# Differential attention on one core: ScalarE's copies ahead of its exponentials, filling work shifted by a quarter, another accumulator for the last item

## The reference

```python
def one_block(args):
    qi, i = args
    sc = jnp.einsum('bqhcd,bkhcd->bhcqk', qi, k).astype(jnp.float32) * scale
    ...
    p = jax.nn.softmax(jnp.where(mask, sc, NEG_INF), axis=-1)
    a = p[:, :, 0] - lam * p[:, :, 1]
    return jnp.einsum('bhqk,bkhv->bqhv', a.astype(v.dtype), v)
...
og = rms_norm(og, gla_norm_w)
yc = (og.reshape(b, l, D_C) * jax.nn.silu(cg.astype(f32))).astype(h.dtype)
...
y = jnp.concatenate([yc, yd], axis=-1) @ w_out
```

## Time and profile before

| | |
|---|---|
| median of 3 runs | 1270.98 us (1270.24 to 1275.65) |
| the profiled execution's own time | 1270.85 us |
| its span (first to last instruction) | 1269.1 us |
| TensorE busy | 1215.1 us, 96% of the span |
| VectorE busy | 883.4 us, 70% |
| GpSimd busy | 735.7 us, 58% |
| ScalarE busy | 292.1 us, 23% |
| mean granted TensorE clock | 0.988 |

### The profile page before, as it was taken

How to read it: one execution, slowest core, us unless ns; L and a number is a source line. 1 busy time by engine, 2 the same in 40 slices (tenths; PEclk the granted TensorE clock), 3 DMA queues, 4 the chain that set the end, 5 groups by cost and what they waited for, 6 DMA issues and landing times.

```text
span 1269.1 us, 23149 instructions
## 1 busy us (share of the span) xinstructions
PE 1215.1 (96%) x8605; PEld 1150.3 (91%) x8605; DVE 883.4 (70%) x1294; ACT 292.1 (23%) x626; POOL 735.7 (58%) x566
## 2 busy tenths in 40 slices
PE   6969899999999999999999998899999999999995
PEld 6967799999999999999999986799999999999995
DVE  6987588999999941217544688767999999972222
ACT  3015332222222200003111166423222222210002
POOL 6732257676677676666653441256666666666661
PEclk9989899999999999999999999999999999999998
DMA  6310022322322223224222311132322222233221
GB/s 213 117 59 28 26 84 83 100 83 83 96 86 83 90 93 100 91 91 129 84 84 67 102 51 35 34 111 84 98 85 83 93 89 83 86 96 100 88 77 72
DMA packets 35556, 108.92 MB, mean 86 GB/s; under 512 B 5984, under 2 KB 7824, under 8 KB 35504
## 3 DMA queue, kind: packets, MB, share of 16 engines
q1 hardware_dynamic: 29232, 102.51, 25.2%
q10 hardware_dynamic: 6272, 5.67, 1.5%
HBM read 103.04 MB, written 5.13 MB: 85 GB/s over the span
## 4 chain that ended last, share of the span: by engine, by line
PE 88%; DVE 8%; ACT 2%; issue 1%; DMA 0%; POOL 0%; POOLq 0%; ACTq 0%; SPq 0%; DVEq 0%
PE psum L450 18%; PE psum L448 12%; PE psum L449 12%; PE psum L451 11%; PE psum L452 9%; PE psum L437 7%; PE psum L439 7%; PE psum L438 6%; DVE even_winsum L1429 1%; PE psum L789 1%; PE psum L656 1%; DVE small L1650 1%; DVE even_rope_swapped L1411 1%; DVE probs L1500 1%; ACT diff_probs L1142 0%
## 5 line engine op out<-in xcount | busy, mean ns | idle before, releaser
L398 POOL TENSOR_TENSOR w_lo<-w_raw,w_hi 128x1024 fp32r<-128x1024 f32 x187 | 485.9, 2598 | 15.6
L395 POOL TENSOR_TENSOR tick<-tick 1x1 f32<-1x1 f32 x183 | 53.4, 292 | 479.0 <-PE psum L439 240.2
L450 PE MATMUL psum<-h_both,w_hi 128*128 128x480 f32 x704 | 267.1, 379 | 0.0
L448 PE MATMUL psum<-h_both,w_hi 128*128 128x304 f32 x704 | 216.0, 307 | 0.0
L449 PE MATMUL psum<-h_both,w_hi 128*128 128x304 f32 x704 | 212.9, 302 | 0.0
L451 PE MATMUL psum<-h_both,w_lo 128*128 128x304 f32 x704 | 211.0, 300 | 0.0
L396 POOL TENSOR_SCALAR w_hi<-w_raw 128x1024 fp32r<-128x1024 f32 x187 | 197.5, 1056 | 9.5 <-DMA w_raw<-in_weights 8.1
L437 PE MATMUL psum<-h_both,w_hi 128*128 128x272 f32 x608 | 181.2, 298 | 13.6 <-DVE h_both L1241 9.8
L452 PE MATMUL psum<-h_both,w_lo 128*128 128x240 f32 x704 | 191.6, 272 | 0.0
L439 PE MATMUL psum<-h_both,w_lo 128*128 128x272 f32 x608 | 177.1, 291 | 0.0
L438 PE MATMUL psum<-h_both,w_hi 128*128 128x272 f32 x608 | 176.3, 290 | 0.0
(11 more groups left out here) (238 smaller groups left out, 2399.4 us busy)
## 6 DMA issues: line engine op xcount, KB each, us to landing
w_raw<-in_weights SPq DMA_DIRECT2D x187, 512.0 KB, 3.5
x<-in_x SPq DMA_DIRECT2D x8, 272.0 KB, 5.5
out_y<-x SPq DMA_DIRECT2D x8, 272.0 KB, 2.4
out_diff_v_new<-odd_dv ACTq DMA_DIRECT2D x1, 1024.0 KB, 5.3
out_diff_k_new<-odd_kT ACTq DMA_DIRECT2D x1, 1024.0 KB, 4.7
even_rope<-in_rope ACTq DMA_DIRECT2D x1, 544.0 KB, 3.8
odd_rope<-in_rope ACTq DMA_DIRECT2D x1, 544.0 KB, 3.7
consts<-in_consts ACTq DMA_DIRECT2D x1, 384.5 KB, 4.9
```

The costliest lines, as they stand in the source:

```text
L395: pool.tensor_tensor(tick[:, :], tick[:, :], tick[:, :], ALU.mult).then_inc(ticks, 1)
L398: pool.tensor_tensor(w_lo[:, k], w_raw[:, k % RAW], w_hi[:, k].bitcast(F32), ALU.subtract).then_inc(w_ready, 1)
L448: pe.matmul(one, wh, both[:, 0, 0:ONE], start=first, stop=False)
L450: pe.matmul(two, wh, both[:, :, ONE:T], start=first, stop=False)
```

## The change

It has four parts.

- ScalarE: in unit `u` the loop now issues `odd_turned(u)` and then `odd_exp(u + 1)`. Before it issued `odd_exp(u + 1)` in unit `u - 1`, ahead of `odd_turned(u)`.
- TensorE: the filling work of units 9 and later is one step further on. Units 9 to 19 now hold one step at each place. A half chunk ends at place 0 of units 9, 11, 13, 15, 17 and 19, ahead of `odd_scores(u + 2)`, and the next one begins at place 1 of the same unit, behind the scores. Before, it ended at place 1 and the next began at place 0 of the unit after. The step of item 10 (m = 6) that unit 19 takes up is missing behind the loop.
- VectorE: `out_first` now stands between `odd_normalise(u + 1)` (and `head_copy`) and `odd_max(u + 2)`; it stood at the end of the unit.
- The last half chunk (m = 7) goes to accumulator 0 and waits for no `x_upd`; `head_low(4)` stands ahead of its `out_first`.

```diff
         ODD_FILL = {-1: (0, 8), 0: (1, 2), 1: (1, 2), 2: (1, 1), 3: (1, 3), 4: (1, 3), 5: (1, 3), 6: (1, 3),
-                    7: (1, 1), 8: (0, 1), 9: (0, 1)} | {u: (1, 1) for u in range(10, 20)}
+                    7: (1, 1), 8: (0, 1)} | {u: (1, 1) for u in range(9, 20)}
...
-        assert done == 0 and item == 10
+        assert done == 1 and item == 10
...
                     if m == 0:
                         pe.wait_ge(evac, EVEN_IN + ODD_IN)
-                    else:
+                    elif m < KC - 1:
                         pe.wait_ge(x_upd, X_ODD + m)
...
-                    ins = tiles(3, s, [(4 * (m % 2) + c, y_hi[:, c], y_lo[:, c])], c == 0, c == 3)
+                    ins = tiles(3 if m < KC - 1 else 0, s, [(4 * (m % 2) + c, y_hi[:, c], y_lo[:, c])], c == 0, c == 3)
...
             odd_values(19)
-            gla_fill(6, 0, 4)
+            gla_fill(6, 1, 4)
...
             for u, (b, h) in enumerate(OU):
                 odd_turned(u)
+                if 1 <= u < len(OU) - 1:
+                    odd_exp(u + 1)
...
-                if u + 2 < len(OU):
-                    odd_exp(u + 2)
...
                 if h == 0 and b >= 1:
                     head_copy(b - 1)
+                if fill_end.get(u, 0) >= 4:
+                    out_first(S_ODD_OUT, fill_end[u] - 4, KC)
                 if u + 2 < len(OU):
                     odd_max(u + 2)
...
-                if u in fill_end:
-                    if fill_end[u] < 4:
-                        gate_in(fill_end[u])
-                    else:
-                        out_first(S_ODD_OUT, fill_end[u] - 4, KC, 0)
+                if fill_end.get(u, 4) < 4:
+                    gate_in(fill_end[u])
             head_copy(4)
-            out_first(S_ODD_OUT, 6, KC, 0)
+            out_first(S_ODD_OUT, 6, KC)
             head_scale(4)
+            head_low(4)
             out_first(S_ODD_OUT, 7, KC, 0)
-            head_low(4)
```

More of the change, by code:

```diff
@@ L1257, in add_out, with out_first @@
                 ve.tensor_tensor(halves(x[:, m]), halves(x[:, m]), pair(acc), ALU.add).then_inc(x_upd, 1)
-            def out_first(s0, m, mid0, upd0):
-                if m >= 0:
-                    add_out(slab_done if m % 2 else mid_done, (s0 if m % 2 else mid0) + m // 2 + 1, 3, m)
+            def out_first(s0, m, mid0, acc=3):
+                add_out(slab_done if m % 2 else mid_done, (s0 if m % 2 else mid0) + m // 2 + 1, acc, m)
             def out_norm(s0, mid0, n, early):
@@ L1515, in _ @@
                 if u in EVEN_FILL:
-                    out_first(S_EVEN_OUT, EVEN_FILL[u], 0, 0)
+                    out_first(S_EVEN_OUT, EVEN_FILL[u], 0)
                 if c == 0 and b >= 1:
@@ L1521, in _ @@
             for m in range(len(EVEN_FILL), KC):
-                out_first(S_EVEN_OUT, m, 0, 0)
+                out_first(S_EVEN_OUT, m, 0)
             even_low(4)
```

## The result

The changed kernel takes 1276.88 us (median of 22 runs, 1273.47 to 1279.3). In the same sessions the kernel before takes 1273.24 (22 runs, 1270.24 to 1276.6); its first three runs, shown above, had a median of 1270.98. The ratio is 1.0022, 95% interval 1.0013 to 1.0031: slower by about 2.8 us (the two medians are 3.64 apart, inside the interval), which is real and lies within the 0.5% that I called no change.

What follows compares the result with a forecast made beforehand. TensorE, busy 96%, was taken as the bound, with 10.7 us of waits in the stage. 6.6 us lost less 2.45 gained in the tail, added to 1270.85, gave 1275.0; 0.6 for the clock made 1275.6, range 1270.0 to 1280.0.

Steps and rivals of the forecast that it cites:

- ScalarE's order: Copy of unit u ahead of unit u+1's exponentials: 4.21 us a unit instead of 4.74; alone a gain of 1.7 us.
- The fill and `out_first`: At the middle of odd units, `out_first` waits behind normalisation and stalls TensorE: 10.0 us a pair of units against 9.5.
- The collision: In unit 11, GpSimd's split (L398) holds VectorE's L1665 until 793.6, so TensorE stalls 4.2 us.
- the second rival: No collision: L1665 starts ahead of L398 in unit 11; 2.2 us less, no long stall, 1272.3; chance 0.25.
- The clock: Behind the 4.2 us stall TensorE's clock may fall: bounds 0 and 1.6 us, 0.6 taken.
- the stepping: Row lengths followed through all units in the new order; for the old kernel it gave `out_chunk` at 834.0 against 833.86.
- The tail: From unit 19's transposes to `out_chunk`: 10.0 us instead of 12.45, a gain of 2.45.
- The sum: First `out_chunk` 4.15 us later (6.6 - 2.45), giving 1275.0; with 0.6 for the clock, 1275.6.
- The third rival: Stalls of 4.2 and 2.4 us each lower TensorE's clock, 1.6 us each: 1278.2, slower by over 0.5%; chance 0.2.

Runs made afterwards that it cites:

- after_old_act: The changed kernel with ScalarE's old order (exponentials two units ahead, in front of the copy): ratio 1.0016 to the kernel before.
- after_kept_busy: The changed kernel with unit 10's value product repeated six times in unit 11, where TensorE waits for `out_first(1)`: ratio 1.0038 to the kernel before.
- last_only: The kernel before with the last half chunk in accumulator 0, no `x_upd` wait, and `head_low(4)` ahead of its addition: ratio 0.9989.
- before_narrow_split: The kernel before with GpSimd's low part of a split done on 128 of 1024 columns for slabs beyond the first four: ratio 0.9879.

## Why the prediction held

**ScalarE's order.** Right: 1.7 us forecast, 0.9987 measured alone, and waits for the copy down from 4.8 to 0.4. I took it as additive with the fill; after_old_act makes that doubtful. The interval of 0.9987 reaches from a gain of 0.3 us to one of 3.1, so that the figure agrees to the digit is luck.

**The fill and `out_first`.** Right, place by place. The waits for `x` came to 9.3 where I said "some 10", each at the middle of an odd unit, the longest in unit 11, 4.07 against 4.2; VectorE waits for L1142 ahead of each reciprocal. `out_first(1)` started at 793.51 against the 793.67 stepped. First transposes, stepped and measured:

| unit | 12 | 13 | 14 | 15 | 16 | 17 | 18 | 19 | `out_chunk` |
|---|---|---|---|---|---|---|---|---|---|
| stepped | 795.39 | 799.60 | 807.11 | 811.32 | 815.93 | 819.66 | 825.37 | 828.02 | 838.02 |
| measured | 795.86 | 801.32 | 807.97 | 812.16 | 817.68 | 821.07 | 825.93 | 828.51 | 838.32 |

**The collision.** Right for unit 11, where the second rival (L1665 ahead of L398) was decided by 0.24 us: 790.64 for L398, 790.88 for L1664. The rule of the Trainium skill (SBUF — State Buffer, "SBUF: two separate sides") that I weighed is that who starts first holds the ports for its whole instruction. The trace agrees: L1664, second by 0.24 us, lasted until L398 was over, and `out_first`, which reads PSUM, took its usual 0.70 at 815.91 beside L398 from 815.89 to 818.25. What I left out is a second hold: beside the first part of a split, L396 at 814.78, L1664 of 160 columns took 1.19 us at 814.79 instead of 0.37.

**The clock.** The size at the place was wrong and the sum right. Behind the stall the slow clock cost 0.64 ahead of unit 12's transposes and 1.25 up to unit 13's, 1.9 together, beyond my upper bound of 1.6 for one fall. But a stall can take in a delay ahead of it: from unit 12 to 14 the stepping has 4.21 + 7.51 = 11.7 us, and the trace has 12.1. Over the whole stage the stepping without the clock gives 838.02 - 738.21 = 99.8 and the trace 100.4, the 0.6 that I had added. That this agrees is partly luck, since errors elsewhere cancelled: unit 15 to 16 took 0.9 more than stepped, with the hold by L396, and units 16 to 18 took 1.2 less. With the clock kept up, after_kept_busy has 4.20 + 7.46 for these units, which is the stepping's.

**The tail.** The wait of 1.5 is gone and no head chain took its place. Alone this is worth 1.4 us by the ratio (last_only). From unit 19's transposes to `out_chunk` are 838.32 - 828.51 = 9.81, against 12.45 before: a gain of 2.6, forecast 2.45. Some 0.9 of either is the fill step that was done early.

**The sum.** Forecast 4.75 us later than the profiled execution of before, measured 4.37 between the two profiled ones and 4.78 in the stage. The ratio over 22 runs each, 1.0022, puts it lower, at 1.7 to 3.9 us: the two profiled executions are nearer to my sum than the whole of the runs is, and my 4.75 lies above that interval. The median of 1276.88 can't be held against my 1275.6 either, since before's own median is 2.3 us higher over the 22 runs than over the three I had added to. What held is the way of the change, its place and its being under 0.5%; its size I put some 2 us too high. The third rival (two long stalls that each cost 1.6) did not come: the stalls behind unit 11's are 1.6 and 1.9 us.

Two figures of the working are wrong without harm to it. The second rival's 1272.3 doesn't follow from its terms: 1275.0 less 2.2 is 1272.8. And a gain of over 0.5% would need 6.4 of the 10.7 us of waits, not nearly all.

## What to carry to other kernels

- Where an in-order engine serves two customers, ask of each wait not only when its input is ready but what stands ahead of it in that queue. `out_first` had its data when VectorE was idle, and still came 1.9 us later in unit 13 and 4.3 in unit 11, because a reciprocal that waited for someone else stood ahead.
- Step through the waits with row lengths, in the old order first until it gives the old time, then in the new. Parts that gain apart can be measured apart: here two of three gained 4.7 us together, and the third lost 3.7 alone and 7.5 on top of them, so the sum of parts measured alone was not the whole either.
- Before two traces are compared stage by stage, look at the clock in both, window by window, and at where each execution stands among its kernel's times. Falls of the clock worth 1.5 us stood in some traces here and not in others, as large as the parts that were measured.
- A repair of one wait can hand the time to the next customer of the same engine, and to the clock. Look at the sum of TensorE's waits, not at the wait that was repaired.

## What the runs showed that I had not expected

The narrow split made the kernel before 1.2% faster, where I had stepped 5 us of 1273. In the profiled executions, 10.4 us apart, 6.4 us of it lie ahead of the stage (the first gate wait ends at 731.79 instead of 738.21), 3.95 in it and 0.1 behind. Of the 3.95 some are the clock's, which before has at 0.66 from 775 to 780 and before_narrow_split at 1.00. The page of before_narrow_split, beside the earlier trace rows:

```profile
PE 1211.0 (96%) x8605; PEld 1148.1 (91%) x8605; DVE 587.3 (47%) x1294; ACT 291.9 (23%) x626; POOL 354.8 (28%) x566
```

VectorE's instructions are the same and as many, yet its busy time fell from 883 to 587 us: a third of what the page shows as VectorE's work went away with GpSimd's shorter instructions, so a high busy share of VectorE can be time in which its instructions are held. The smallest are held too: a TENSOR_SCALAR of 32x2 elements took 1.23 us at 817.05 in the changed kernel, beside L398, instead of 0.16.
